# Moving the second group of modulation row products behind the second up chunk

## The reference

```
m = SiLU(cond) @ mod_w + mod_b      # 1024 -> 9 * 1024, for two conditions (context, latent)
h = RMSNorm(x) * (1 + scale1) + shift1
x += 1/2 * gate1 * (silu(h @ w1) * (h @ w3)) @ w2       # first feed-forward, width 2816
h = RMSNorm(x) * (1 + scale_m) + shift_m
x += gate_m * W_out [attention | gated conv | DeltaNet | Fourier](h)
x += 1/2 * gate2 * SwiGLU_2(RMSNorm(x) * (1 + scale2) + shift2)
```

## Time and profile before

| | |
|---|---|
| three runs, median (lowest to highest) | 3383.18 us (3373.24 to 3384.57) |
| profiled execution, its own time | 3371.52 us |
| span of the profile, first to last instruction | 3369.8 us |
| PE busy | 3081.8 us, 91% of the span |
| PEld busy | 2876.3 us, 85% |
| DVE, ACT, POOL busy | 44%, 24%, 8% |
| mean granted clock of PE | 0.937 of full speed |

### The profile page before, as it was taken

One profiled execution on the slowest core, in us unless ns is written; L12 is line 12 of the kernel. 1 busy time (PEld: TensorE's weight loads), 2 busy tenths in 40 slices (PEclk: granted clock), 3 DMA queues, 4 the chain that ended last, 5 costly groups with the idle time before them and its releaser, 6 DMA issues.

```text
span 3369.8 us, 58553 instructions
## 1 busy us (share of the span) xinstructions
PE 3081.8 (91%) x24855; PEld 2876.3 (85%) x24855; DVE 1467.9 (44%) x2406; ACT 803.2 (24%) x1155; POOL 253.3 (8%) x305
## 2 busy tenths in 40 slices
PE   5999999897779989999989999989876998999997
PEld 3999999894578788999989999989745888999997
DVE  3333444415355553343355444451433654544444
ACT  2222211322322232212223222222322223322221
POOL 2000000100022100000010000010001321000001
PEclk6999999997779999999999999999966899999998
DMA  6345322121000125434421222212200002122221
GB/s 237 102 161 170 131 76 84 51 63 38 0 4 4 39 69 169 163 130 142 149 75 38 75 75 75 75 63 76 72 4 2 4 3 76 38 75 75 75 75 44
DMA packets 163107, 258.95 MB, mean 77 GB/s; under 512 B 11868, under 2 KB 130884, under 8 KB 162592
## 3 DMA queue, kind: packets, MB, share of 16 engines
q1 hardware_dynamic: 140960, 174.57, 15.8%
q0 software_dynamic: 22016, 82.46, 7.3%
HBM read 253.85 MB, written 3.15 MB: 76 GB/s over the span
## 4 chain that ended last, share of the span: by engine, by line
PE 63%; issue 24%; DMA 5%; DVE 5%; ACT 1%; POOLq 1%; DVEq 1%; POOL 1%; ACTq 0%
PE ps L561 43%; PE ps L548 17%; DMA PT<-mod_w 4%; PE ps L584 1%; POOLq L438 1%; PE ps L808 1%; DMA ub<-mixer_tables 0%; DVE ast L1599 0%; DVE pexp L1608 0%; DVE PT L1365 0%; DVEq L1366 0%; POOL dB L524 0%; PE ps L852 0%; DVE cv L1566 0%; DVE PT L1645 0%
## 5 line engine op out<-in xcount | busy, mean ns | idle before, releaser
L561 PE MATMUL ps<-hh,uh 128*128 128x320 f32 x3744 | 864.3, 312 | 58.7 <-DVE hl L1392 48.6
L561 PE MATMUL ps<-hl,uh 128*128 128x320 f32 x3744 | 858.2, 311 | 0.0
L561 PE MATMUL ps<-hh,ul 128*128 128x320 f32 x3744 | 857.4, 310 | 0.0
L561 PEld LDWEIGHTS ps<-hh,uh 128*128 128x128 f32 x3744 | 629.6, 189 | 80.5 <-issue 69.1
L561 PEld LDWEIGHTS ps<-hl,uh 128*128 128x128 f32 x3744 | 631.0, 189 | 0.0
L561 PEld LDWEIGHTS ps<-hh,ul 128*128 128x128 f32 x3744 | 630.6, 189 | 0.0
L1357 DVE TENSOR_TENSOR ul<-raw,uh 128x1024 fp32r<-128x1024 f32 x322 | 390.6, 1235 | 270.9 <-ACT uh L1060 255.2
L1402 DVE SCALAR_TENSOR_TENSOR xT<-ps,modT,xT 128x128 f32<-128x128 f32 x736 | 371.5, 547 | 302.5 <-PE ps L561 301.3
L1060 ACT CAST uh<-raw 128x1024 fp32r<-128x1024 f32 x322 | 323.7, 1046 | 480.4 <-PE ps L561 420.9
L1422 DVE SCALAR_TENSOR_TENSOR PT<-ps,PT 128x640 f32<-128x640 f32 x88 | 72.5, 824 | 776.6 <-PE ps L561 776.6
L561 PE MATMUL ps<-gh,uh 128*128 (+1 forms) x1408 | 325.0, 312 | 15.2 <-DVE ul L1357 14.3
(11 more groups left out here) (241 smaller groups left out, 2507.8 us busy)
## 6 DMA issues: line engine op xcount, KB each, us to landing
raw<-ffn_w SPq DMA_DIRECT2D x264, 512.0 KB
PT<-mod_w POOLq DMA_DIRECT2D x72, 1024.0 KB, 6.2
raw<-w_in SPq DMA_DIRECT2D x40, 512.0 KB
raw<-w_out SPq DMA_DIRECT2D x8, 768.0 KB
ub<-mixer_tables POOLq DMA_DIRECT2D x2, 2176.0 KB, 8.3
out<-PT SPq DMA_DIRECT2D x5, 512.0 KB, 2.6
PT<-x_sample SPq DMA_DIRECT2D x4, 512.0 KB, 6.9
raw<-w_out SPq DMA_DIRECT2D x16, 128.0 KB
```

The source lines that it names most:

```text
L561: last = pe.matmul(pair(q)[:, lo:hi], wt[:, wk * P:(wk + 1) * P], mv(mk, lo, hi), start=start and i == 0 and p_ == 0, stop=stop and i == n ...
```

## The change

In the blocks with modulation PE's program is written in another order. Before, the second group of row products stood between the two products of the second up chunk (the argument `between` of `up`). Now it stands behind both of them, directly in front of the column products. Nothing else is changed: the same instructions, waits, transfers and buffers, and the code of the other engines is the same.

```diff
                         n = i + (first - 1)
                         pe.wait_ge(acc_used.sem, acc_used.at(l, abase + 8 * i - 8))
                         modulation_rows(ml, 2 * n, 0)
-                        up(i, 1, lambda: modulation_rows(ml, 2 * n + 1, 1))
+                        up(i, 1)
+                        modulation_rows(ml, 2 * n + 1, 1)
                         modulation_cols(ml, n)
                         down(i - 1, n)
```

## The result

The changed kernel takes 3402.11 us (median of 4 runs, 3400.12 to 3404.53) against 3380.66 for the kernel before: a ratio of 1.007 with a 95% interval of 1.005 to 1.009, about 21 us slower where 19.6 were worked out. The profiled execution has a span of 3400.3 us.

The account below looks back on a forecast made before the run. PE, busy 91% of the span, was taken as the bound. Added 20.2 (copy wait) plus 19.5 (clock falls) less 20.1 removed gives 19.6 us: 3391 from the profiled execution, 3398 from the mean of four; range 3376 to 3412.

Parts of the forecast that it names:

- The wait for the copy: Between rows and columns, PE waits for ACT's copy, formerly beside a product: 1.26 us per block, 20.2 us added.
- the clock falls: Behind wait and columns, 2.96 us together, 13 of 16 blocks lose the clock at 1.5 us each: 19.5 us added.
- the removed side: What moving the second row group saves: slice waits 17.2, product interruption 1.6, one clock fall 1.3, together 20.1 us.
- waits for `mod_w`: PE's idle time before row products whose weight slices land late; all 17.2 us taken as gone.
- interruption: A product following row products starts slowly, 0.1 us in each of 16 blocks; 1.6 us taken as removed.
- one clock fall: Second feed-forward's first block: a wait was followed by a granted clock below 1.00; 1.3 us taken as removed.
- no third wait: Sign: the prediction is wrong if PE meets a third wait between the rows and the second down chunk.
- The 16 falls: By the skill's rule of a fall at every wait, all 16 blocks would lose the clock: 24 us instead of 19.5.
- The step that failed: Fall count: 2.96 us lies 0.8 of the way from the wait keeping the clock to the one losing it; 13 blocks.
- The clock holding: Rival: column products count as work for the clock, only the swap of waits is left, 3374 to 3379 us; chance 0.22.
- The loads did not stay late: Rival, that slices take over 14 us and half the old waits stay: 8.6 us over forecast, 3407; chance 0.03.
- The faster case: Rival: the median execution's extra 12 us are `mod_w` waits and clock falls, which go too: 3371 us; chance 0.07.

Follow-up runs that it names:

- the second time: The changed kernel measured again, nothing altered: 3399.38 us, ratio 1.0078 to the kernel before.
- the kernel with the rows in the middle of a product: Kernel before, with the second group of row products behind 4 of 8 chunks of the second up chunk's second product: 3357.99 us, ratio 0.9952.
- The eight wide matmuls: Changed kernel plus 8 unused wide matmuls per block between row and column products, filling PE's wait for ACT's copy: 3375.74 us, ratio 0.9996 to the kernel before.
- the two-part copy: Changed kernel with ACT's copy split by group, the first group's rows copied early, behind the second chunk's SiLU: 3357.08 us, ratio 0.9943 to the kernel before.

## Why the prediction was right, point by point

From the first row products of the first block to those of the last one in each of the two feed-forwards, 14 blocks, the kernel before took 296.39 + 395.79 = 692.18 us and the changed one 303.76 + 406.09 = 709.85: 1.26 us per block, 20.2 in 16, where the prediction's sum is 19.6. The wait for the copy and the clock falls hold by themselves, the removed side only as a whole:

| term (us in 16 blocks) | predicted | measured |
|---|---|---|
| waits for `mod_w`, interruption, one clock fall, removed | 20.1, of which 1.6 is the interruption | 20.8, scaled from 14 blocks: 49.44 on average (692.18 / 14) against 48.14 where nothing is late |
| wait for the copy, added | 20.2 | 20: blocks without a fall 49.35 to 49.42, less 48.14 to 48.15 |
| clock falls | 13 of 1.5 | 14 (13 the second time) of 1.53: 50.88 less 49.35 |

The interruption of a product by the rows, 0.1 us in each block, did not go; it moved. Columns that stand behind a product took 1.70 us; behind the wait they take 1.81 (139.20 to 141.01), and the 48.14 us are those of the kernel with the rows in the middle of a product, which still has the interruption. Without this term 18.5 us were worked out as removed, 2.3 less than the table has; where the rest comes from isn't shown, and that 20.1 was met is in this part luck.

**The mechanism.** The path over ACT's copy (16 waits of 1.13 to 1.21 us), the vanished waits for the slices and the clock at 0.50 across the first down products are all in the profile of after as foretold, and there is no third wait. The Trainium skill (TensorE: Matmul & The Clock Gate, section "HAM oscillation — how this bites in real kernels") tells of a clock that falls anew at every wait between bursts of matmuls, and puts these waits at some 3 to 5 us. The 16 falls that the prediction drew from it went too far, since the waits here are shorter and have column products behind them; 14 and 13 were measured.

**The step that failed.** The number of falls came from a line between a wait of 2.49 us, behind which the clock had stayed, and one of 3.08, behind which it had not. The two were not alike, since behind the longer one stood eight matmuls with a stationary operand only 14 wide (128*14 in the earlier trace rows). It gave 13, but its reason was wrong, so that the count was met by luck: with 0.50 us of waiting and the columns, 2.31 us together, the clock fell 14 times, and with wait and columns parted by 0.6 us of work 12 times. The 2.49 us of the earlier trace rows were no safe length, and one stretch does not have one fate: equal blocks kept the clock or lost it. The assumption that columns do not hold the clock up was right.

**The rivals.** The clock holding was ruled out by the measurement. The eight wide matmuls show what it would have been worth, 0.9996 of the time before, and the two-part copy what comes with the wait gone as well. The loads did not stay late. The faster case had one sound part: waits and falls of that kind can be had back, 16 to 19 us, but only by a version that covers the copy. Its premise, that the 12 us between two executions of the kernel before are such waits, isn't shown: with the rows in the middle of the product the executions still lie between 3355.50 and 3367.12, and the profiled one has neither waits nor falls in its blocks.

**The profiles' spans.** They differ by 30.5 us, about 10 more than the blocks explain. The same 600 us of the span, which lie in the mixer and outside the blocks, from the kernel before, the changed one and the one with eight matmuls:

```profile
620.00:1220.00 600.00, 519.87 (x5273) 448.00 (x5272) 269.73 (x524) 157.29 (x278) 70.58 (x89) 0.88 0.12 37
```

```profile
620.00:1220.00 600.00, 528.88 (x5297) 458.57 (x5298) 267.82 (x528) 159.16 (x281) 69.88 (x89) 0.86 0.10 31
```

```profile
620.00:1220.00 600.00, 518.41 (x5328) 448.51 (x5328) 279.08 (x543) 162.41 (x287) 70.61 (x89) 0.89 0.11 37
```

The mixer's code is the same in all three and its clock differs. The execution profiled with eight matmuls took 3354.40 us, where the median of its 12 runs is 3375.74, although its blocks are as long as those of the changed kernel without a fall. The times of these 12 go with the granted clock of the whole execution: 0.944 in the fastest of the 12 (3354.40), 0.932 in the slowest (3381.36). So single executions of one kernel can lie up to 27 us apart; medians carry the comparison, and the blocks its explanation. Why the mixer's clock differs from one execution to the next was not tried.

## What to carry to other kernels

Before moving work next to its consumer, price the hop over the other engine that used to lie beside other work (here 1.2 us for signal, copy and signal), and place it so that a piece of independent work still covers the hop: half a product here, or half of the consumer itself. When two light stretches of PE become neighbours, take their idle time and their narrow matmuls together, and ask the granted clock, block by block, what that does. Filling matmuls are a cheap test, if they fill the whole wait: eight did here, three did not. A wait that a profile shows is worth its length only if what replaces it on the path is shorter.

## What the runs showed of the hardware that was not expected

- Matmuls with two moving columns did not hold the clock: 32 of them in one piece, without a wait, lost it in 15 of 16 blocks, and in 8 of these for twice the usual 3.4 us; 16 of them behind wide matmuls, 1.70 us, lost it in none of the 16 blocks of the kernel before.
- The same blocks kept their clock 16 times of 16 with the wait filled by eight wide matmuls and lost it 14 times of 16 with three; 0.6 us of wide matmuls between the wait and the columns did not save it (12 of 16).
- Equal blocks did not fare equally: the same wait and the same columns lost the clock in 14 blocks of the changed kernel and kept it in two.
- More work made the kernel faster: 128 matmuls whose results nobody reads took about 25 us off the changed kernel.
